# Splitting the first weights of each next head's projection beside the last unit of the present one, with the last looped head written out

## The reference, cut to what matters

```python
def mixer(h, ...):                       # h = rms_norm(x), T x 1024
    proj = h @ w_in                      # 1024 x 4096
    aq, ak, av, hq, hff, hfb, hi, hg = split(proj)
    # 4 attention heads: two softmaxes per head, subtracted, times v
    att = rms_norm(diff_attention(aq, ak, av, lam))
    # 4 recurrent heads (HGRN2), forward and backward, gated
    hgo = rms_norm(o_f + o_b) * silu(hg)
    return concat(att, hgo) @ w_out
x = x + mixer(rms_norm(x))
x = x + expert_choice_ffn(rms_norm(x))   # 16 experts, router, gate, up, down
y = rms_norm(x)
```

## Time and profile before

| | us |
|---|---|
| median of 3 runs | 2280.71 (2280.4 to 2280.78) |
| the profiled execution | 2278.43 |
| its span, from the first to the last instruction | 2276.5 |
| TensorE busy | 2024.2 (89%) |
| VectorE busy | 1461.5 (64%) |
| ScalarE busy | 1108.2 (49%) |
| GpSimd busy | 257.0 (11%) |
| mean granted TensorE clock | 0.951 |

### The profile page before, as it was taken

The page is one execution under the profiler, slowest core; times in us unless marked ns, Lnnn a source line. Parts: engine busy times, 40 slices in busy tenths (PEclk is TensorE's granted clock), DMA queues, the critical chain, the costliest instruction groups (busy, mean ns, idle before and its releaser), DMA issues. The chain is left out here.

```text
span 2276.5 us, 44180 instructions
## 1 busy us (share of the span) xinstructions
PE 2024.2 (89%) x16048; PEld 1763.4 (77%) x16048; DVE 1461.5 (64%) x2748; ACT 1108.2 (49%) x1972; POOL 257.0 (11%) x398
## 2 busy tenths in 40 slices
PE   6999998899897899788899389999999999999990
PEld 5777776677776677566788289999999999999990
DVE  4376576666666467566338857777777777777763
ACT  4322222455555423266323156666666666666652
POOL 2001101000000011100122001111111111111101
PEclk9999999999998999799899689999999999999995
DMA  5211110100002111211233177777777777777756
GB/s 167 81 31 34 29 30 16 37 19 23 19 5 79 51 57 55 75 51 47 102 111 111 49 265 255 245 261 245 260 247 259 246 254 252 255 252 254 253 154 244
DMA packets 181872, 311.99 MB, mean 137 GB/s; under 512 B 11648, under 2 KB 81792, under 8 KB 181760
## 3 DMA queue, kind: packets, MB, share of 16 engines
q1 hardware_dynamic: 168832, 276.87, 36.3%
q0 software_dynamic: 7040, 25.17, 4.9%
q10 hardware_dynamic: 5888, 8.39, 1.0%
HBM read 276.83 MB, written 33.55 MB: 136 GB/s over the span
## 5 line engine op out<-in xcount | busy, mean ns | idle before, releaser
L2128 DVE TENSOR_TENSOR we_lo<-raw,we_hi 128x1024 fp32r<-128x1024 f32 x384 | 466.1, 1224 | 204.5 <-ACT we_hi L2074 203.6
L2040 PE MATMUL psum<-x_parts,we_hi 128*128 128x384 f32 x2048 | 586.3, 360 | 3.1 <-DVE we_lo L2128 3.1
L2042 PE MATMUL psum<-x_parts,we_lo 128*128 128x192 f32 x2048 | 513.9, 251 | 0.0
L2074 ACT CAST we_hi<-raw 128x1024 fp32r<-128x1024 f32 x384 | 400.3, 1054 | 174.5 <-PE psum L2042 101.7
L2042 PEld LDWEIGHTS psum<-x_parts,we_lo 128*128 128x128 f32 x2048 | 392.7, 192 | 0.6
L2040 PEld LDWEIGHTS psum<-x_parts,we_hi 128*128 128x128 f32 x2048 | 386.1, 189 | 4.1 <-issue 3.5
L587 PE MATMUL psum<-hT_hi,w_hi 128*128 128x512 f32 x512 | 215.7, 421 | 12.5 <-DVE w_lo L567 12.5
L589 PE MATMUL psum<-hT_hi,w_lo 128*128 128x512 f32 x512 | 203.1, 397 | 0.0
L588 PE MATMUL psum<-hT_lo,w_hi 128*128 128x512 f32 x512 | 202.9, 396 | 0.0
L587 PE MATMUL psum<-hP_hi,w_hi 128*128 128x512 f32 x256 | 111.0, 434 | 22.7 <-DVE w_lo L567 22.7
L587 PEld LDWEIGHTS psum<-hT_hi,w_hi 128*128 128x128 f32 x512 | 97.6, 191 | 34.3 <-DVE land L1100 7.5
(11 more groups left out here) (297 smaller groups left out, 3849.4 us busy)
## 6 DMA issues: line engine op xcount, KB each, us to landing
raw<-in_w_gate SPq DMA_DIRECT2D x128, 512.0 KB, 5.5
raw<-in_w_up SPq DMA_DIRECT2D x128, 512.0 KB, 6.0
raw<-in_w_down SPq DMA_DIRECT2D x128, 512.0 KB, 4.6
w_raw<-in_w_in SPq DMA_DIRECT2D x96, 256.0 KB, 2.8
y_rows<-x SPq DMA_DIRECT2D x12, 512.0 KB, 2.6
h_rows<-h SPq DMA_DIRECT2D x12, 512.0 KB, 2.9
y<-y_rows SPq DMA_DIRECT2D x12, 512.0 KB, 6.9
w_raw_s<-in_w_in SPq DMA_DIRECT2D x16, 256.0 KB, 3.0
```

The lines of the kernel that those rows point to most:

```text
L2040: pe.matmul(out[:, 0:2 * SLOTS], w_hi[:, s, at], x_parts[p][:, k, :, :], start=(k == 0), stop=False, skip_group_check=True)
L2042: mm = pe.matmul(out[:, SLOTS:2 * SLOTS], w_lo[:, s, at], x_hi[p][:, k, :], start=False, stop=(k == DT - 1), skip_group_check=True)
L2074: act.copy(w_hi[:, n % PARTS, :], raw[:, s, :]).then_inc(hi.sem, 1)
L2128: dve.tensor_tensor(w_lo[:, n % PARTS, :], raw[:, n % RAW, :], w_hi[:, n % PARTS, :].bitcast(F32), ALU.subtract).then_inc(lo.sem, 1)
```

## The change

`heads` now loops over two heads and writes the third out, with numbers in place of the loop's register. ("split", 0) is left out at the start of a head. Instead, right behind the first matmuls of a projection's last unit, the step ("split", 0) of the next projection is placed: of head i+2 in the loop, of the first attention head in the written-out recurrent head (`then`), of head 1 in `opening`, `joined` and `crossing`. The very first split of each recurrent kind (in `opening` and in `crossing`) stays where it was. SyncE's program is unchanged.

```diff
-        def heads(body, steps):
-            with eng.Fori(0, HEADS - 1) as i:
-                for step in steps:
-                    body(step, i, i + 1)
+        def heads(body, steps, units, then=None):
+            for lone in (False, True):
+                with ExitStack() as loop:
+                    i = HEADS - 2 if lone else loop.enter_context(eng.Fori(0, HEADS - 2))
+                    for step in steps:
+                        if step != ("split", 0):
+                            body(step, i, i + 1)
+                        if step == ("unit", units - 1, 0, 0):
+                            if not lone:
+                                body(("split", 0), i, i + 2)
+                            elif then:
+                                then(("split", 0), None, 0)
...
             if kind == "h":
                 h[0](step, None, 0)
+                if step == ("unit", h_s.proj.units - 1, 0, 0):
+                    h[0](("split", 0), 0, 1)
...
-            heads(h[g], hs.stages[1])
+            heads(h[g], hs.stages[1], hs.proj.units, a[g])
             for kind, step in joined[g]:
                 if kind == "h":
                     h[g](step, HEADS - 1, None)
-                elif kind == "a":
+                elif kind == "a" and step != ("split", 0):
                     a[g](step, None, 0)
-                else:
+                elif kind == "o":
                     tile(step)
-            heads(a[g], ats.stages[1])
+                if kind == "a" and step == ("unit", ats.proj.units - 1, 0, 0):
+                    a[g](("split", 0), 0, 1)
+            heads(a[g], ats.stages[1], ats.proj.units)
...
                         h[1](step, None, 0)
+                        if step == ("unit", h_p.proj.units - 1, 0, 0):
+                            h[1](("split", 0), 0, 1)
```

## The result

The changed kernel took 2255.39 us (median of 4 runs, 2254.63 to 2258.92), the kernel before beside it 2280.56 us (median of 4). The ratio is 0.9888, with a 95% interval of 0.9874 to 0.9902: 25.2 us faster, where 14.0 were forecast and a range of 7.7 to 22.8. The sign was right, the size was not. Of all executions behind this document one, of the variant written_alone, was odd: it took 4020.79 us, the others of that kernel 2277.25 to 2285.13, and it is left out of its median and ratio.

What follows compares the result with a forecast made beforehand. The prediction took TensorE as the bound, its standing still being kernel time. Returned waits of 6.0 + 2.55 + 1.6 + 3.75 = 13.9 us, taken as 14.0, moved the median from 2280.71 to 2266.7 us; range 2258 to 2273.

Steps and rivals of the forecast that it cites:

- The sum of the waits: TensorE's waits at the starts of projections in all four kinds of heads: 13.9 us returned, taken as 14.0.
- sample, recurrent: Sample's recurrent heads: two places return their whole 2.09 us, the loop's way back 1.8; 6.0 us in sum.
- prompt, recurrent: Prompt's recurrent heads: 0.65 of 2.09 us returned twice, 1.25 of 2.40 on entry; 2.55 us in sum.
- sample, attention: Sample's attention heads: 0.45 us lost in the first iteration, 0.4 gained in the second, 1.6 in the written head; sum 1.6.
- prompt, attention: Prompt's attention heads: 2.4 us returned into the loop, about 0.3 in its second iteration, 1.05 in the written head; sum 3.75.
- The attention heads: Attention loops: the 1.28 us table load now stands before the exp and begins only when the exp's input is there.
- The way back: Sample's recurrent loop: queued work covers TensorE's 3.69 us branch; 0.3 us estimated behind it, 1.8 of 2.09 returned.
- The entry from `crossing`: Entry into the prompt's recurrent heads: bank free at 782.76, TensorE started at 784.15, so 1.25 of 2.40 us returns.
- The banks of the prompt: Prompt's recurrent heads: G and the next head's tile 0 share a bank, so a 1.4 us wait for G's landing remains.
- The clock returns more: Rival, chance 0.12, 2262 us: clock falls behind TensorE's waits go too, two places at 1.4 us each.
- The slow rival: Chance 0.05, 2295.6 us: TensorE waits for code in the four written-out heads, up to 3.7 us a fetch, eight costing 29.6.

Runs made afterwards that it cites:

- written_alone: Against the kernel before: last looped head of each kind written out, every first split left at its old place; 2281.01 us, ratio 1.0001.
- table_waits: Changed kernel with the two waits of the attention loops' first exp in the other order; 2262.39 us, ratio 0.9912 to the kernel before.
- recurrent_written: Changed kernel with all three heads of each recurrent kind written out, no loop left there; 2249.90 us, ratio 0.9861 to the kernel before.
- two_banks: Changed kernel with the prompt's recurrent heads written out, their tiles on banks 6 and 7 by turns; 2255.48 us, ratio 0.9882 to the kernel before.

## Why the prediction was wrong, point by point

**The sum of the waits: right in size, in part by luck.** 13.9 us were forecast, 13.8 us less standing still were measured, over two profiles before and three after. But its parts were off. The third column has single waits and stage lengths of the first two profiles, the fourth only standing still, from unit 0 to unit 0, as the difference of the means of all five:

| kind | forecast | at the places | standing still by stage | how the places were read |
|---|---|---|---|---|
| sample, recurrent | 6.0 | 5.3 | 4.5 | waits 2.09, 2.09 gone, 2.09 to 1.02 |
| prompt, recurrent | 2.55 | 1.9 | 1.8 | 2.40 to 1.75, 2.09 to 1.41, 2.09 to 1.50 |
| sample, attention | 1.6 | 3.8 | 3.4 | stage lengths 1.67 and 1.72 less, 0.45 less behind the third boundary |
| prompt, attention | 3.75 | 5.2 | 4.3 | 2.56 gone, standing 1.06 less, length 1.55 less |

The fourth column adds up to 14.0. The places add up to 16.2, since lengths have busy time in them and since waits came up elsewhere, as the two for VectorE's keys above. The recurrent kinds returned 2.3 us less than forecast and the attention kinds 2.4 more: two errors cancel in the sum.

**The attention heads: a wrong step.** It is the sentence "In this trace a table load in front of an exp begins only when the exp's input is there". It was read from written-out code and carried to a loop, where the load has no wait. With the load hidden "the sample's attention heads would give about 4 us", the prediction said; they gave 3.8 by the stages' lengths and 3.4 of standing still. table_waits put the assumed wait in and lost 1.2 us an iteration. The load did move to the exp, in the loops alone, and the rule of the Trainium skill on placement per block (ScalarE activation tables: per-element evaluation and per-set limits, Table sets in the compiler and the runtime) agrees with that; it does not decide whether the load costs anything.

**The way back: undersized.** Forecast 0.3 us behind the branch, measured 1.02, 0.69 and 0.70 in three profiles. The branch took 3.41 to 3.78 us in the two profiles of the kernel before and 4.21, 3.87 and 3.89 in the three of the changed one; as the wait for the low part no longer covered it, its end set the start. The prediction had the bound (nothing returned at this place) but took a value near the other end. The fetch rule of the Trainium skill (Runtime: NRT & Kernel Launch, Instruction fetch mechanics) agrees with this loop and with recurrent_written, and again not with the attention loop, whose branch took 0.24 us.

**The entry from `crossing`: a wait overlooked.** 1.25 of 2.40 us were to return, since the bank is free at 782.76. Unit 0 is queued behind the step "start", which waits for the last mix, and 0.65 came back (0.50 in the other two profiles). The rule to ask what is late next was applied to the bank only.

**The banks of the prompt: right.** Waits of 1.41 and 1.50 us for G's landing stand where 1.4 was forecast, and two_banks takes them away.

**The clock: the mechanism right, its term and its chance wrong.** This is the step that failed. The sum put the clock at nothing, and the rival "The clock returns more" had two places at 1.4 us and a chance of 0.12, with the argument "only two of twelve waits were followed by it". That was one execution. Over four profiles with the old splits 12 of 24 recurrent boundaries were throttled, and the entry at 981 in all four; with the moved splits 3 of 60 and none of 10. So a kernel with the old splits has on average 3 stretches and 1 more behind these waits, one with the moved splits 0.3: 3.7 stretches of 1.6 us, **6 us**, as an estimate. The busy time fell by 11.7 us in the means of the profiles. Of these 5.1 us lie in the three stages behind 98, 830 and 981 us, 1.1 in three attention heads at full clock, 1.6 between 609 and 712 us, 2.5 behind 1046 us, the rest here and there.

13.8 and 6 us make 19.8, which the range still held. The other 6 us of busy time carried the time out of it. The medians of 4 and 6 executions (25.2 and 26.8 us) say that they belong to the change as a whole; by which path they come stays open, as throttled stretches far from the moved splits come and go in all kernels.

**The slow rival: fell.** No written-out head has a wait of TensorE of the kind it described. Two waits over 1 us are not named by an engine there, 2.63 us at 910.77 and 1.08 at 914.82; the first stands in the kernel before too (2.57 at 922.88), against the prediction's word that all waits in `joined` are named. TensorE began 0.10 and 0.08 us after the keys that it needs were done, GpSimd's at 910.67 and VectorE's at 914.74, so they are waits for keys and not for code; written_alone stands at 1.0001 and recurrent_written is the faster for it.

## What to carry to other kernels

A wait of 2 us on TensorE can cost more than itself where the clock tends to fall behind it: price such waits with the chance of a throttled stretch, taken from several profiles of the same kernel and not from one. Split a result into standing still and busy time, since the first repeated within 1.5 us here and is what a change of order acts on; a short wait can still vanish under a throttled stretch. Before a wait is carried from one place of the code to another, read which instruction holds it: in a loop and in straight code the same two lines put it on different ones.

## What the runs showed of the hardware

- Behind waits of 2.0 to 2.6 us of TensorE the granted clock fell in 16 of 28 cases, behind the wait of 1.7 to 1.9 us in front of 784 in 3 of 10, behind those of 0.2 to 1.6 us at the other boundaries in none. One fall cost 1.6 us.
- The same loop branch of TensorE took between 3.35 (written_alone) and 4.21 us from one kernel and execution to the next, in the loop with some 2490 TensorE instructions from unit 0 to unit 0. In the loops with some 1250, 900 and 330 it took 0.21 to 0.25 us. In the same code written out no wait for code is seen.
- Executions of one kernel differ by up to 14.5 us (2251.2 to 2265.7, and 2273.2 to 2286.7), while the time that TensorE stands still differed by 1.5 us at most in the profiles of one kernel.
